# Scaling x inside the turn of x, and a later schedule around it, in a one-core mLSTM and attention block

## What is computed

```
h     = x * rsqrt(mean(x*x) + eps) * pre_w            # per token
proj  = h @ w_in                                      # 1024 x 12296 columns
mlstm = chunkwise scan over 8 chunks of 128 tokens, 4 heads, from silu(conv(q, k)), v, o
hm    = norm(mlstm) * silu(z);   att = three dilated window attentions, 4 heads
y     = (sigmoid(g_m) * (hm @ w_pm) + sigmoid(g_a) * (att @ w_pa)) @ w_out
out   = x + y * rsqrt(mean(y*y) + eps) * post_w
```

## Time and profile before

| | |
|---|---|
| median of 3 runs | 1407.75 us (1406.2 to 1410.4) |
| profiled execution | 1408.32 us, its span 1406.5 us |
| PE busy | 1363.8 us (97%) |
| DVE / ACT / POOL busy | 790.5 / 643.9 / 582.2 us |
| mean granted TensorE clock | 0.985 |
| chain that ended last | PE 90% of the span |

### The profile page before, as it was taken

One profiled execution on the slowest core, in us unless ns is written; L12 is line 12 of the kernel. 1 busy time (PEld: TensorE's weight loads), 2 busy tenths in 40 slices (PEclk: granted clock), 3 DMA queues, 4 the chain that ended last, 5 costly groups with the idle time before them and its releaser, 6 DMA issues.

```text
span 1406.5 us, 18724 instructions
## 1 busy us (share of the span) xinstructions
PE 1363.8 (97%) x6436; PEld 1133.2 (81%) x6436; DVE 790.5 (56%) x1253; ACT 643.9 (46%) x1321; POOL 582.2 (41%) x408
## 2 busy tenths in 40 slices
PE   7799999999999999999999999999999997999898
PEld 5588888888888888878888888888888886887686
DVE  6755337345543845957666665765543444766532
ACT  6544544543454455345445445444554554334221
POOL 3434345335443534544435344444434552355300
PEclk8999999999999999999999999999999999999899
DMA  6113133323333323463443434434443248856221
GB/s 188 45 42 99 41 74 106 94 51 100 97 83 70 94 65 69 135 185 124 111 141 84 163 124 111 154 94 141 116 149 109 78 159 291 278 164 229 85 91 60
DMA packets 211358, 165.02 MB, mean 117 GB/s; under 512 B 33296, under 2 KB 187440, under 8 KB 211264
## 3 DMA queue, kind: packets, MB, share of 16 engines
q1 hardware_dynamic: 211264, 163.81, 39.3%
HBM read 117.41 MB, written 40.08 MB: 112 GB/s over the span
## 4 chain that ended last, share of the span: by engine, by line
PE 90%; DVE 3%; issue 2%; DMA 2%; ACT 2%; SPq 1%; POOL 0%; DVEq 0%; POOLq 0%; ACTq 0%
PE proj L1207 68%; PE proj L1169 5%; PE proj L1147 2%; PE keep L1252 2%; PE bank L1231 2%; PE keep L1308 2%; PE bank L1317 2%; PE bank L1240 1%; PE bank L1280 1%; PE bank L1313 1%; PE bank L1263 1%; DMA raw<-w_pa 1%; DMA x_sb<-x_in 1%; DVE pm_sb L1720 1%; DMA out_raw<-w_out 1%
## 5 line engine op out<-in xcount | busy, mean ns | idle before, releaser
L1060 POOL TENSOR_TENSOR w_lo<-raw,w_hi 128x512 fp32r<-128x512 f32 x164 | 232.1, 1415 | 447.4 <-ACT w_hi L1409 447.4
L1207 PE MATMUL proj<-hi_T,w_hi 128*128 128x512 f32 x832 | 339.7, 408 | 14.7 <-ACT snap L1427 7.0
L1207 PE MATMUL proj<-hi_T,w_lo 128*128 128x512 f32 x832 | 326.8, 393 | 0.0
L1207 PE MATMUL proj<-lo_T,w_hi 128*128 128x512 f32 x832 | 326.0, 392 | 0.0
L1207 PE MATMUL proj<-hi_B,w_hi 128*128 128x512 f32 x624 | 255.7, 410 | 4.1 <-DVE lo_B L1987 3.9
L1207 PE MATMUL proj<-hi_B,w_lo 128*128 128x512 f32 x624 | 244.9, 392 | 0.0
L1207 PE MATMUL proj<-lo_B,w_hi 128*128 128x512 f32 x624 | 244.5, 392 | 0.0
L1060 POOL TENSOR_TENSOR w_lo<-s_sb,w_hi 128x512 fp32r<-128x512 f32 x104 | 154.3, 1486 | 177.8 <-ACT w_hi L1409 177.5
L1207 PEld LDWEIGHTS proj<-hi_T,w_hi 128*128 128x128 f32 x832 | 157.4, 189 | 49.4 <-issue 12.1
L1207 PEld LDWEIGHTS proj<-hi_T,w_lo 128*128 128x128 f32 x832 | 157.3, 189 | 34.6
L1207 PEld LDWEIGHTS proj<-lo_T,w_hi 128*128 128x128 f32 x832 | 157.7, 190 | 30.6
(11 more groups left out here) (239 smaller groups left out, 2035.5 us busy)
## 6 DMA issues: line engine op xcount, KB each, us to landing
raw<-w_in SPq DMA_DIRECT2D x95, 512.0 KB, 6.0
m_spill<-stage SPq DMA_DIRECT2D x16, 1024.0 KB, 6.1
chunk<-m_spill SPq DMA_DIRECT2D x32, 512.0 KB, 3.7
gate_spill<-stage SPq DMA_DIRECT2D x8, 1024.0 KB, 4.1
gst<-gate_spill SPq DMA_DIRECT2D x32, 256.0 KB, 3.1
share<-share_spill SPq DMA_DIRECT2D x12, 512.0 KB, 4.7
x_sb<-x_in SPq DMA_DIRECT2D x8, 512.0 KB, 6.9
hm_spill<-stage SPq DMA_DIRECT2D x4, 1024.0 KB, 8.9
```

Source lines behind the costliest of these rows:

```text
L1060: TT(w_lo_ring[k % RING][:], src, w_hi_ring[k % RING][:].bitcast(F32), ALU.subtract).then_inc(lo_pool, 1)
L1207: mm = pe.matmul(acc(p, which), w[:, kt, :], m[:, kt, :], start=(first and kt == 0 and w is wh and m is h_hi[b]), stop=(kt == 3 and w is w ...
```

## The change

Seven edits: (1) x is not scaled by VectorE and not transposed; GpSimd writes `diag[t]`, the identity times the tile's factors, and TensorE multiplies x by it in fp32. (2) At the start, four of the eight turns of the second half come before product 1 rather than two, high parts of coming weights are made earlier, and S4 is formed after T4. (3) `conv` of the second tile moves from 7p+11 to 7p+12, all that hangs on it by one step, the spill to 7p+17, and the first `chunk_in` of a head to 172, 200, 235, 270. (4) Around W0 the loads of hm move from W0-2..W0 to W0..W0+2, behind the gate loads, and sums, high and low parts by one to four steps. (5) `out_lo` goes from GpSimd to VectorE, `out_hi` and `out_lo` come later. (6) `merged_hi/lo(0, 1)` join the lists at NK. (7) Output tile 0 takes its eight row blocks in the outer loop and the two halves in the inner one.

```
-        ready = 7 * pair_of["mo", h] + 10
+        ready = 7 * pair_of["mo", h] + 11
...
-            for j, a in ((1, 7), (0, 11)):
+            for j, a in ((1, 7), (0, 12)):
...
-            sp_late[at + 16].append(("spill", p))
+            sp_late[at + 17].append(("spill", p))
...
-    for at, b in ((W0 - 2, "B11"), (W0 - 2, "B21"), (W0 - 1, "T1"), (W0, "B22")):
-        sp_late[at].append(("hm_in", b))
...
+            act_late[W0 + 1 + at].append(("hm_hi", b, i))
...
+    for at, b, i in ((1, "T1", 0), (1, "T1", 1), (2, "T2", 0), (2, "T2", 1), (2, "T3", 0), (3, "T3", 1),
+                     (4, "T4", 0), (4, "T4", 1)):
+        dve_late[W0 + at].append(("hm_sum", b, i))
...
+    for at, b in ((0, "B11"), (0, "T1"), (0, "B22"), (2, "B21")):
+        sp_late[W0 + at].append(("hm_in", b))
...
-            act_late[at + 2].append(("out_hi", i, j))
-            pool_late[at + 2].append(("out_lo", i, j))
+            act_late[min(at + 4, NK)].append(("out_hi", i, j))
+            dve_late[(at + 4, NK - 1, NK, NK)[i]].append(("out_lo", i, j))
...
+    act_late[NK].append(("merged_hi", 0, 1))
+    dve_late[NK].append(("merged_lo", 0, 1))
...
                 TT(ssq[:, NT + t:NT + t + 1], ssq[:, t:t + 1], halfneg[:, 0:1], ALU.pow).then_inc(x_rs, 1)
+                g.wait_ge(x_rs, t + 1)
+                nc.gpsimd.tensor_scalar(diag[:, t, :], ident[:], ssq[:, NT + t:NT + t + 1], None, ALU.mult
+                                        ).then_inc(x_norm, 1)
...
+                if t == 0:
+                    for kt in range(KT):
+                        if kt == 6:
+                            pe.wait_ge(mg_lo, 2)
+                        pe.wait_ge(w_out_lo, kt + 1)
+                        for half in range(2):
+                            mm = rows_of_w_out(kt, half)
...
-                    mm = pe.transpose(ht1_bank[kt][:, t * P:(t + 1) * P], x_sb[:, t, kt * P:(kt + 1) * P], ident[:])
+                    mm = pe.matmul(ht1_bank[kt][:, t * P:(t + 1) * P], x_sb[:, t, kt * P:(kt + 1) * P], diag[:, t, :],
+                                   start=True, stop=True)
...
-                for kt in {0: (0, 4), 1: (1, 5, 2, 6, 3, 7)}.get(k, ()):
+                for kt in {0: (0, 4, 1, 5), 1: (2, 6, 3, 7)}.get(k, ()):
...
-                dve.wait_ge(x_rs, t + 1)
-                TS(x_sb[:, t, :], x_sb[:, t, :], ssq[:, NT + t:NT + t + 1], None, ALU.mult).then_inc(x_norm, 1)
...
             sums_and_low("T3", third_sum, 8)
+            sums_and_low("T4", fourth_sum, 12)
             add(0, "S4")
-            sums_and_low("T4", fourth_sum, 16)
```

More of the change, by code:

```diff
@@ L286, in hybrid_kernel @@
         dve_late[W0 - 11 + i].append(("att_lo", i))
-    for at, b in ((W0 - 2, "B11"), (W0 - 2, "B21"), (W0 - 1, "T1"), (W0, "B22")):
-        sp_late[at].append(("hm_in", b))
     hm_hi_no, hm_lo_no = {}, {}
-    for at, b in ((0, "B11"), (1, "B21"), (2, "T2"), (2, "T1"), (3, "T3"), (4, "T4"), (5, "B22")):
+    for at, b in ((0, "B11"), (1, "B21"), (3, "T2"), (3, "T1"), (4, "T3"), (5, "T4"), (6, "B22")):
         for i in range(2):
             hm_hi_no[b, i] = len(hm_hi_no) + 1
[L293 to L300, removed]
+            act_late[W0 + 1 + at].append(("hm_hi", b, i))
+    for at, b, i in ((1, "T1", 0), (1, "T1", 1), (2, "T2", 0), (2, "T2", 1), (2, "T3", 0), (3, "T3", 1),
+                     (4, "T4", 0), (4, "T4", 1)):
+        dve_late[W0 + at].append(("hm_sum", b, i))
+    for at, b, i in ((3, "B11", 0), (3, "B11", 1), (4, "B21", 0), (5, "B21", 1), (5, "T2", 0), (5, "T2", 1),
+                     (6, "T1", 0), (6, "T1", 1), (6, "T3", 0), (7, "T3", 1), (7, "T4", 0), (7, "T4", 1),
+                     (8, "B22", 0), (8, "B22", 1)):
+        hm_lo_no[b, i] = len(hm_lo_no) + 1
+        dve_late[W0 + at].append(("hm_lo", b, i))
     for t in range(KT):
@@ L1159, in output_tile, with rows_of_w_out @@
                 pe.wait_ge(mg_lo, 2 * t + 1 if t < 2 else t + 3)
+                def rows_of_w_out(kt, half):
+                    i, j, columns = kt // 2, kt % 2, half_of(half)
+                    for a, w in ((hi_part, out_hi), (hi_part, out_lo), (lo_part, out_hi)):
+                        mm = pe.matmul(y_slot(t)[:, columns], a[:, kt, :], w[i][:, j, columns],
+                                       start=(kt == 0 and a is hi_part and w is out_hi),
+                                       stop=(kt == KT - 1 and a is lo_part))
+                    return mm
+                if t == 0:
[5 more added lines that the diff above has]
+                            mm = rows_of_w_out(kt, half)
+                            if kt == KT - 1:
+                                mm.then_inc(pe_y, 1)
+                    return
                 for half in range(2):
-                    columns = half_of(half)
                     for kt in range(KT):
[L1163 to L1168, removed]
-                            mm = pe.matmul(y_slot(t)[:, columns], a[:, kt, :], w[i][:, j, columns],
-                                           start=(kt == 0 and a is hi_part and w is out_hi),
-                                           stop=(kt == KT - 1 and a is lo_part))
+                        if t == 1 and kt == 6:
+                            pe.wait_ge(mg_lo, 4)
+                        mm = rows_of_w_out(kt, half)
                     mm.then_inc(pe_y, 1)
@@ L1348, in second_half @@
                     pe.wait_ge(x_norm, 5 + t)
-                    mm = pe.transpose(b[:, t * P:(t + 1) * P], x_sb[:, 4 + t, kt * P:(kt + 1) * P], ident[:])
+                    mm = pe.matmul(b[:, t * P:(t + 1) * P], x_sb[:, 4 + t, kt * P:(kt + 1) * P], diag[:, 4 + t, :],
+                                   start=True, stop=True)
                 mm.then_inc(pe_ht, 1)
@@ L1489, in _ @@
                 first_half(kt)
-            for j in range(4):
-                second_half(j)
-                h_high("T2", j, 2 * j + 2)
-                if j == 0:
-                    after(0)
-                elif j == 1:
-                    high(2)
-                    high(3)
+            second_half(0)
+            second_half(1)
+            h_high("T2", 0, 2)
+            after(0)
+            second_half(2)
+            h_high("T2", 1, 4)
+            high(2)
+            second_half(3)
+            h_high("T2", 2, 6)
+            high(3)
+            h_high("T2", 3, 8)
             for j in range(4):
@@ L1500, in _ @@
             high(4)
+            after(2)
             for j in range(4):
-                if j == 2:
-                    after(2)
                 h_high("T3", j, 9 + j)
             high(5)
-            for j in range(4):
-                h_high("B22", j, 8)
+            high(6)
             after(4)
@@ L1510, in _ @@
                 h_high("T4", j, 13 + j)
-            high(6)
+            for j in range(4):
+                h_high("B22", j, 8)
             ACT_EARLY, HIGH_EARLY = (2, 4), 6
@@ L1871, in tail_piece @@
                     merged_low(*it[1:])
+                elif what == "out_lo":
+                    i, j = it[1:]
+                    dve.wait_ge(w_out_hi, 2 * i + j + 1)
+                    TT(out_lo[i][:, j, :], out_raw[i][:, j, :], out_hi[i][:, j, :].bitcast(F32), ALU.subtract
+                       ).then_inc(w_out_lo, 1)
             def combine(h, part):
@@ L1974, in late_square, with mean_square @@
                                        op0=ALU.mult, op1=ALU.add, accum_out=ssq[:, t:t + 1]).then_inc(x_sq_late, 1)
-            def scale(t):
-                if t < 6:
-                    dve.wait_ge(x_sq, t + 1)
-                    TS(ssq[:, t:t + 1], ssq[:, t:t + 1], EPS, None, ALU.add).then_inc(x_ms, 1)
-                dve.wait_ge(x_rs, t + 1)
-                TS(x_sb[:, t, :], x_sb[:, t, :], ssq[:, NT + t:NT + t + 1], None, ALU.mult).then_inc(x_norm, 1)
+            def mean_square(t):
+                dve.wait_ge(x_sq, t + 1)
+                TS(ssq[:, t:t + 1], ssq[:, t:t + 1], EPS, None, ALU.add).then_inc(x_ms, 1)
             def first_low(kt):
```

26 lines of the change are left out of this document (10 added, 16 removed).

## The result

The changed kernel takes 1399.91 us (median) where the kernel before took 1408.32 us beside it: a ratio of 0.9943, with a 95% interval from 0.9925 to 0.996. The profiled execution of 1400.15 us has a span of 1398.4 us. I had forecast 1390 from 1376 to 1401: the sign is right and the time is inside the range, but of the 18.5 us that I expected only 8.1 came between the two profiled executions. The time lies outside the bounds of the forecast itself (1383 to 1397); the range holds it only because it reached up for rivals B and C, and neither of them is what happened, so that part is luck.

What follows compares the result with a forecast made beforehand. TensorE bounds the kernel, busy 1363.8 of 1406.5 us, so only its waits and own work count. Terms -8 - 6.8 + 11.4 + 5.8 - 9.7 - 11.2 = -18.5 on 1408.3 us gave 1389.8, said as 1390, range 1376 to 1401.

Steps and rivals of the forecast that it cites:

- B: Rival at the start: it gives nothing, as open products, slow GpSimd and a lower clock eat the 8 us; 1398, 12%.
- C: Rival at the WHOLE products: hm's loads are late and they wait after all, by 6 to 8 us; 1397, 7%.
- Last steps: Last product steps and output tile 0: P4 starts earlier and tile 0 ends at 1313.3, not 1324.5; -11.2 us.
- WHOLE: WHOLE products: the third no longer waits for `pa_done`; 8.0 us of wait and 1.8 of slow clock go; -9.7 us.
- later steps hold 4.8 us of VectorE work per 5.5: WHOLE products: after two tight `pa_done`, VectorE's work was claimed to fit, 4.8 us per 5.5.
- First chunks: First chunk of each head: its load behind weights on SyncE makes TensorE wait, +11.4 us, plus +5.8 of clock.
- Start: Start: VectorE's stretch to B22's low parts is the bound and ends at 60.6; P3 of pair 0 near 61.5; -8 us.
- P4 then ends near 56: Start: P4's 3.86 us wait goes, so P4 ends near 56 and 16 gate matmuls not needing B22 before 60.
- Convolution: Near 600 us: the copy P4 needs comes before `conv`; a 3.88 us wait and 2.9 of clock go; -6.8 us.
- A: Rival at the first chunks: they come in time because the queue is emptier, the +17.2 falls away; 1372.6, 11%.
- D: Rival at the first chunks: slower, the four waits longer than any landing shows; at 8 us mean wait 1416; 5%.
- the rule of the Trainium skill that I cited: Start: transposes do not hold TensorE's clock as matmuls do; product 0 would take 2.7 us, not 4.7; sum at most 0.7 lower.

Runs made afterwards that it cites:

- this part alone: The kernel before with only the new plan of the WHOLE products (hm's loads, high parts, sums, low parts later): 1405.08 us, ratio 0.9981.
- the tail alone: The kernel before with only the edits to w_out's high and low parts, merged part 1 and output tile 0: 1396.84 us, ratio 0.9922.
- The two experiments on this turn: On the changed kernel: hm's low parts later in VectorE's order, 1396.17 us; GpSimd's first pm S1 held until VectorE's first six hm low parts, 1400.98 us.
- The kernel with the chunk ahead of the weights: The changed kernel with each head's first chunk load issued ahead of the same step's weights on SyncE: 1383.60 us, ratio 0.9831.
- the start alone: The kernel before with only the changed start (diagonal products and the new order): 1402.15 us, ratio 0.9954.
- the diagonal products alone: The kernel before with GpSimd's diagonals and fp32 products replacing VectorE's scaling and the transposes, old order of the start: 1405.53 us, ratio 0.9978.
- the convolution alone: The kernel before with only the three shifts of the convolution stage (conv, spill and first chunk one step later): 1422.66 us, ratio 1.0107.

## Why the prediction was right in sign and wrong in size

**Last steps and WHOLE, the step that failed (4.5 us of the 10.4).** My terms -9.7 and -11.2 came true, as -9.5 (-8.6 with this part alone) and, with the tail alone, -10.7. What failed was one sentence in the WHOLE part: "later steps hold 4.8 us of VectorE work per 5.5". Three things were wrong with it. It took each operation of 1.18 us at its length with GpSimd idle, while the three groups of low parts from 1211.93 to 1228.9 took 14.3 us for eight, where 9.4 was due. It left no room for the backlog that the late loads had made by 1191.57, though the landings themselves came as forecast, 12.1 us after the first WHOLE product where I had 11.8. And it looked for the next late thing only inside the WHOLE products, where none was, and not at the first product behind them, which waits for the seventh and eighth gated product. The two experiments on this turn show that the order makes the wait: another order removes it, another place for one collision does not.

**First chunks (1.8 us).** The waits are 3.42, 1.34, 3.97 and 3.26 where I had 2.8, 1.1, 4.1 and 3.4. So 0.6 us of the miss are waits, and 1.2 the clock: 19.0 us of loss less 12.0 of waits leave 7.0, where I had 5.8, 2.9 for each of two heads. By the start of each head's next chunk it was 1.7, 0.1, 2.9 and 1.75 for heads 0 to 3, and 0.5 elsewhere. That the sum is near is partly luck: head 3 cost less than my 2.9 and head 0, which I had named as open, made up for it. I had read 2.9 behind one wait and taken it for every long one, though the kernel before has a cheaper case, my own 1.8 behind its 7.82 us. The kernel with the chunk ahead of the weights confirms that its place behind them makes the waits, by taking them away.

**Start (1.9 us).** P3 started at 63.86 (forecast 61.5, which I had rounded to a gain of 8). The T2 sums ended at 35.3 (forecast 34.9) and VectorE's B22 parts at 60.5 (60.6). "P4 then ends near 56" failed: it ended at 58.4, since GpSimd's `w_lo` and S1 met T4's sums, not S4; 24 gate matmuls of 0.23 lie behind it, and there was nothing left to hide them. I had placed the 1.7 us of collision in the stretch without asking which of its parts TensorE wants first. A diagonal took 0.61 us where I had 0.45; this moved product 0 little: it started at 18.70, not 18.0, at ScalarE's pace.

**Convolution (0.5 us).** Forecast -6.8, read as -6.3 in the changed kernel (the 2.9 of the table and head 0's wait of 3.42) and about -6 alone. My last worry, that a later silu makes TensorE wait elsewhere, did not come true: there is no such wait.

**Attention (1.3 us), open.** No edit touches it. The eight profiled executions with diagonal products lose 0.6 to 1.7 us there against the kernel before, the five without them at most 0.6; two waits of 0.5 us are in the changed kernel's list. I did not find why.

**The rivals.** A (the chunks in time) is what another order in SyncE's queue makes true, and only that. B (a start that gives nothing) fell with the 5.7 us of the start alone, C (hm's loads late) with their landing as forecast, D with waits that never passed 4.0 us.

## What to carry to other kernels

When a change moves work of an engine later, add up that engine's list up to the first consumer behind the stage, not to the stage's end, and put each operation at its length beside the other engine's work. A DMA that something waits for goes ahead of a bulk load of the same step. The terms that were read from rows of the same tile and queue came out within an eighth, but for the waits of heads 0 and 1 (3.42 and 1.34 for 2.8 and 1.1) and the clock behind them; the large misses lie in the sentences that said that nothing else is late.

## What the runs showed of the hardware

VectorE and GpSimd stretch each other by whole instructions. Low parts of 128 x 1024 take 1.18 us alone and 2.28 beside GpSimd (4.55 for two), and GpSimd's of 128 x 512 take 1.28 alone and up to 2.27. The Trainium skill (SBUF — State Buffer, Who interferes with whom) says that the shared port is locked for an instruction and not divided; the trace agrees, about one instruction of the other is added to each. Work on GpSimd is thus not free while VectorE is late, though it was at 41% of the span.

A 128 x 128 `tensor_scalar` on GpSimd has a median of 0.61 us, against the 0.2 that I had worked out as an estimate from the Trainium skill (GPSIMD Engine Reference, 3.1 Elementwise), which gives that rate as a best case: for a tile this small the rate for an element is not what one pays. The 128 x 1 power beside it takes 0.57, with a 128th of the elements.

Product 0 doesn't settle whether transposes hold the clock. After 2.64 us of idle time behind real products the changed kernel ran its first six matmuls at the lower level (1.2 GHz); the diagonal products alone, after 2.61 us behind the same products, ran the first five at the upper one. No run here decides on the rule of the Trainium skill that I cited, nor did it move the sum.

The start differs from execution to execution by up to 3.3 us with nothing edited there (P3 of pair 0 at 69.23 with the tail alone, at 72.54 with the convolution alone). The late start of the latter comes with x's load: ScalarE took the sixth block of x at 14.18 us in the profiled execution of the kernel before, and at 16.43 in that of the convolution part alone, waiting 2.60 us for the load. A difference of 2 us at the start therefore needs the medians and not one trace.
